# Attention in fp32 parts on one core: low score products of 128 rows, single fp32 copies for the value products, and pieces of the next round issued two steps ahead

## What the reference computes

```python
# fox: forgetting attention
logits = einsum('bhqd,bhkd->bhqk', q, k) * scale + F[..., :, None] - F[:, :, None, :]
p = softmax(where(kpos <= qpos, logits, -inf))
out = einsum('bhqk,bhkd->bhqd', p, v)
# stick-breaking attention
z = einsum('bhqd,bhkd->bhqk', q, k) * scale
after = reverse_cumsum(log_sigmoid(-z)) - log_sigmoid(-z)      # where kpos < qpos
out = einsum('bhqk,bhkd->bhqd', exp(log_sigmoid(z) + after), v)
```

## Time and profile before

| | |
|---|---|
| median of 3 runs | 2871.64 us |
| the profiled execution's own time | 2868.15 us |
| its span, first to last instruction | 2866.0 us |
| mean granted TensorE clock | 0.965 |
| TensorE busy | 95% of the span |
| VectorE, ScalarE, GpSimd busy | 55%, 32%, 33% |
| attention, from the first mask product to the last | 1328.6 to 1982.0 us |

### The profile page before, as it was taken

The page is one execution under the profiler, slowest core; times in us unless marked ns, Lnnn a source line. Parts: engine busy times, 40 slices in busy tenths (PEclk is TensorE's granted clock), DMA queues, the critical chain, the costliest instruction groups (busy, mean ns, idle before and its releaser), DMA issues.

```text
span 2866.0 us, 33315 instructions
## 1 busy us (share of the span) xinstructions
PE 2722.8 (95%) x12938; PEld 2207.3 (77%) x12938; DVE 1579.2 (55%) x1505; ACT 908.4 (32%) x1298; POOL 937.7 (33%) x385
## 2 busy tenths in 40 slices
PE   7999999999999899989999999989999999999998
PEld 4878777878787778867777777777778788888876
DVE  5744455666556633565647466554777714551653
ACT  3411034443343410225445555544223301210211
POOL 2555542323233245531101001000454444444442
PEclk9999999999999999999999999975999999999999
DMA  7222221212121343321101010111111111111111
GB/s 300 68 89 82 103 60 59 71 52 78 45 63 59 114 165 95 118 95 45 36 17 37 31 37 31 37 62 78 37 45 51 44 44 46 50 45 50 51 36 74
DMA packets 54884, 193.61 MB, mean 68 GB/s; under 512 B 6472, under 2 KB 10184, under 8 KB 53616
## 3 DMA queue, kind: packets, MB, share of 16 engines
q1 hardware_dynamic: 39648, 141.08, 14.9%
q10 hardware_dynamic: 15120, 50.90, 5.0%
HBM read 157.84 MB, written 29.92 MB: 66 GB/s over the span
## 4 chain that ended last, share of the span: by engine, by line
PE 79%; DVE 11%; ACT 5%; issue 3%; DMA 1%; DVEq 0%; ACTq 0%; SPq 0%; PEldq 0%; POOL 0%; PEld 0%
PE G L238 51%; PE G L1778 7%; PE G L1838 2%; PE U L1814 2%; PE G L1836 2%; PE S L1031 2%; DVE tiles_in L2399 1%; PE G L1898 1%; DVE tiles_in L2401 1%; PE G L1804 1%; PE S L1804 1%; DVE A_lo L2404 1%; PE U L1063 1%; ACT tiles_in L2352 1%; PE G L1803 1%
## 5 line engine op out<-in xcount | busy, mean ns | idle before, releaser
L264 POOL TENSOR_TENSOR w_hi<-w_raw,ones 128x1024 fp32r<-128x1024 f32 (+1 forms) x141 | 342.5, 2429 | 1167.7 <-PE G L238 984.7
L238 PE MATMUL G<-H_hi,w_hi 128*128 128x512 f32 x1744 | 545.5, 394 | 7.4 <-DVE x L1582 4.7
L238 PE MATMUL G<-H_lo,w_hi 128*128 128x512 f32 x1744 | 538.3, 390 | 0.0
L238 PE MATMUL G<-H_hi,w_lo 128*128 128x512 f32 x1744 | 537.5, 389 | 0.0
L238 PEld LDWEIGHTS G<-H_hi,w_hi 128*128 128x128 f32 x1744 | 324.9, 188 | 80.7 <-issue 6.8
L238 PEld LDWEIGHTS G<-H_lo,w_hi 128*128 128x128 f32 x1744 | 327.9, 188 | 68.8
L238 PEld LDWEIGHTS G<-H_hi,w_lo 128*128 128x128 f32 x1744 | 327.7, 188 | 68.9
L269 POOL TENSOR_TENSOR w_lo<-w_raw,w_hi 128x1024 fp32r<-128x1024 f32 (+1 forms) x141 | 374.6, 2657 | 11.0
L1755 POOL TENSOR_TENSOR w_lo<-w_raw,w_hi 128x1024 fp32r<-128x1024 f32 x24 | 63.8, 2658 | 544.4 <-ACT w_hi L1937 544.4
L2148 DVE TENSOR_TENSOR probsT_lo<-U,probsT_hi 128x512 fp32r<-128x512 f32 (+1 forms) x192 | 101.4, 553 | 170.0 <-ACT probsT_hi L1967 169.0
L238 PE MATMUL G<-A_hi,w_hi 128*128 128x512 f32 x512 | 160.0, 394 | 13.0 <-DVE A_lo L2406 13.0
(11 more groups left out here) (408 smaller groups left out, 4677.1 us busy)
## 6 DMA issues: line engine op xcount, KB each, us to landing
w_raw<-w_in SPq DMA_DIRECT2D x65, 512.0 KB, 3.5
w_raw<-w_up SPq DMA_DIRECT2D x44, 512.0 KB, 3.5
pre_raw<-w_in SPq DMA_DIRECT2D x30, 512.0 KB, 3.6
w_raw<-w_out SPq DMA_DIRECT2D x16, 512.0 KB, 3.7
w_raw<-w_down SPq DMA_DIRECT2D x16, 512.0 KB, 3.5
wm<-w_mod SPq DMA_DIRECT2D x6, 1024.0 KB, 17.0
xT<-xT SPq DMA_DIRECT2D x8, 512.0 KB, 19.2
wm<-w_mod SPq DMA_DIRECT2D x2, 2048.0 KB, 23.6
```

The source lines that it names most:

```text
L238: mm = nc.tensor.matmul(dst[:, n * NB:n * NB + c], w[:, k, :], m[:, k, n * NB:n * NB + c], start=first, stop=last)
L264: eng.tensor_tensor(dst, src, ones.unsqueeze(1).to_broadcast([P, kt, P]), ALU.mult)
```

## The change

It has three parts. **Scores:** each head gets a tile of q low of its own, with zeros in the other head's 64 rows, and the low product takes all 128 rows. Four VectorE instructions write the zeros once, ahead of the rounds. **Value products:** the turned weights and v are copied once, as fp32, by ScalarE, and each block takes one fp32 product of 64 columns. `probs_low`, `v_low` and `values_low` go; `out_of` reads PSUM and writes the output in one instruction. The banks of `U` are free once ScalarE has copied them. **Steps:** SHIFT is 2 in place of 6, so pieces and all that goes by n come four steps later; the last 18 steps have no piece.

```diff
-        TILES, STEPS, SHIFT = 2 * TT, 2 * TT * 2 * HEADS, 6
+        TILES, STEPS, SHIFT = 2 * TT, 2 * TT * 2 * HEADS, 2
...
-            return ([take(f"q_hi{n}{h}", [P, T], F32R) for h in range(2)], take(f"q_lo{n}", [P, T], F32R),
-                    [take(f"k_parts{n}{h}", [P, T], F32R) for h in range(2)], take(f"v_parts{n}", [P, TT, 2, 2, HD], F32R))
+            return [take(f"q_hi{n}{h}", [P, T], F32R) for h in range(2)], [take(f"q_lo{n}{h}", [P, T], F32R) for h in range(2)], \
+                [take(f"k_parts{n}{h}", [P, T], F32R) for h in range(2)], take(f"att_v{n}", [P, TT, P])
...
-                use_u(("p", c), ("dve", "p low", c))
+                use_u(("p", c), ("act", "p copied", c))
...
-                    pe.matmul(z[:, cols], QL[own_rows(hh), t], Ks[hh][own_rows(hh), cols], start=False, stop=tt // 4 != b)
+                    pe.matmul(z[:, cols], Ql[hh][:, t], Ks[hh][:, cols], start=False, stop=tt // 4 != b)
...
                 for c, b0, n in GROUP_AT[g]:
-                    S.wait(pe, "act", "p high", c)
-                    S.wait(pe, "dve", "p low", c)
+                    S.wait(pe, "act", "p copied", c)
                     for b in range(n):
-                        k = b0 + b
-                        if k == 0:
-                            pe.matmul(V[:, at:at + P], pTh[c % 2][:, b, :], v[:, k, hh, :, :].rearrange("p a d -> p (a d)"), start=True, stop=False)
-                        mm = pe.matmul(V[:, at:at + HD], pTl[c % 2][:, b, :], v[:, k, hh, 0, :], start=False, stop=tt == 0)
-                        if k:
-                            mm = pe.matmul(V[:, at:at + P], pTh[c % 2][:, b, :], v[:, k, hh, :, :].rearrange("p a d -> p (a d)"), start=False, stop=k == tt)
+                        mm = pe.matmul(V[:, at:at + HD], pT[c % 2][:, b, :], v[:, b0 + b, own_rows(hh)], start=b0 + b == 0, stop=b0 + b == tt)
...
-            def values_low(g4):
...
+            for n in range(2):
+                for hh in range(2):
+                    other = other_rows(hh)
+                    v.tensor_scalar(SETS[n][1][hh][other, :], SC[other, :], 0.0, None, ALU.mult)
...
-            def v_low(r):
...
-            def probs_low(g):
...
-                do("out", v.tensor_tensor(dst, V.rearrange("p (b a d) -> p b a d", a=2, d=HD)[:, :, 0, :], tb, ALU.add), g4)
+                dst, src = ON[:, t0:t0 + 4, own_rows(hh)], V[:, 0:4 * HD].rearrange("p (b d) -> p b d", d=HD)
                 if x == "f":
-                    me("out", g4)
                     do("row sums", v.reciprocal(rs[:, n0:n0 + 4], rs[:, n0:n0 + 4]), g4)
                     me("row sums", g4)
-                    do("head out", v.tensor_tensor(dst, dst, rs[:, n0:n0 + 4].unsqueeze(2).to_broadcast([P, 4, HD]), ALU.mult), g4)
+                    do("out", v.tensor_tensor(dst, src, rs[:, n0:n0 + 4].unsqueeze(2).to_broadcast([P, 4, HD]), ALU.mult), g4)
+                else:
+                    do("out", v.tensor_copy(dst, src), g4)
```

More of the change, by code:

```diff
@@ L1636, in program @@
         SC = take("rstd12", [P, T])
-        pTh = [take(f"probsT_hi{n}", [P, 4, P], F32R) for n in range(2)]
-        pTl = [take(f"probsT_lo{n}", [P, 4, P], F32R) for n in range(2)]
+        pT = [take(f"probsT{n}", [P, 4, P]) for n in range(2)]
         fsum = [take(f"forget_sums{n}", [P, T]) for n in range(2)]
@@ L1649, in program @@
         left = take("left_over", [P, T + 8])
-        tb = take("values_low", [P, 4, HD])
         dump = take("squares_made", [P, P])
@@ L1698, in program @@
                 for half in range(2):
-                    use_u(("v", 2 * (q - 1) + half), ("dve", "v low", 2 * (q - 1) + half))
+                    use_u(("v", 2 * (q - 1) + half), ("act", "v copied", 2 * (q - 1) + half))
             if s > TILES and s % TILES == 2:
@@ L1787, in scores @@
                 r = g // TILES
-                (Qh, QL, Ks, _), z, w = SETS[r % 2], Z[g % 2], (tt + 1) * P
+                (Qh, Ql, Ks, _), z, w = SETS[r % 2], Z[g % 2], (tt + 1) * P
                 if g == 0:
@@ L1820, in values @@
                 _, hh, tt = tile_of(g)
-                r, at = g // TILES, g % 4 * P
+                r, at = g // TILES, g % 4 * HD
                 v = SETS[r % 2][3]
@@ L1827, in values @@
                 if g % TILES == 0:
-                    S.wait(pe, "dve", "v low", 2 * r + 1)
+                    S.wait(pe, "act", "v copied", 2 * r + 1)
                 for c, b0, n in GROUP_AT[g]:
-                    S.wait(pe, "act", "p high", c)
-                    S.wait(pe, "dve", "p low", c)
+                    S.wait(pe, "act", "p copied", c)
                     for b in range(n):
-                        k = b0 + b
-                        if k == 0:
-                            pe.matmul(V[:, at:at + P], pTh[c % 2][:, b, :], v[:, k, hh, :, :].rearrange("p a d -> p (a d)"), start=True, stop=False)
-                        mm = pe.matmul(V[:, at:at + HD], pTl[c % 2][:, b, :], v[:, k, hh, 0, :], start=False, stop=tt == 0)
-                        if k:
-                            mm = pe.matmul(V[:, at:at + P], pTh[c % 2][:, b, :], v[:, k, hh, :, :].rearrange("p a d -> p (a d)"), start=False, stop=k == tt)
+                        mm = pe.matmul(V[:, at:at + HD], pT[c % 2][:, b, :], v[:, b0 + b, own_rows(hh)], start=b0 + b == 0, stop=b0 + b == tt)
                     S.mark("pe", "values", mm, c)
@@ L1853, in out_turned @@
             def out_turned(r):
-                S.wait(pe, "dve", "out" if X[r % 2] == "s" else "head out", 4 * r + 3)
+                S.wait(pe, "dve", "out", 4 * r + 3)
                 for half in range(2):
@@ L1953, in k_high, with v_copied @@
                 S.mark("act", "k high", ins, q)
-            def v_high(r):
+            def v_copied(r):
                 v = SETS[r % 2][3]
@@ L1959, in v_high, with probs_copied @@
                     S.wait(act, "pe", "v turned", 2 * r + half)
-                    src = bank_of_u(("v", 2 * r + half)).rearrange("p (b h d) -> p b h d", h=2, d=HD)
-                    S.mark("act", "v high", act.activation(v[:, 4 * half:4 * half + 4, :, 0, :], src, ACT.Copy), 2 * r + half)
-            def probs_high(g):
+                    S.mark("act", "v copied", act.activation(v[:, 4 * half:4 * half + 4, :], blocks_of(bank_of_u(("v", 2 * r + half)), 4), ACT.Copy), 2 * r + half)
+            def probs_copied(g):
                 for c, _, n in GROUP_AT[g]:
@@ L1966, in probs_high @@
                     S.wait(act, "pe", "values", c - 2)
-                    S.mark("act", "p high", act.activation(pTh[c % 2][:, 0:n, :], blocks_of(bank_of_u(("p", c)), n), ACT.Copy), c)
+                    S.mark("act", "p copied", act.activation(pT[c % 2][:, 0:n, :], blocks_of(bank_of_u(("p", c)), n), ACT.Copy), c)
             def not_taken(g):
@@ L1984, in probs @@
                 S.mark("act", "made", act.activation(p, p, ACT.Exp, scale=-1.0, bias=mn[:, g % 2, :], accum_out=rs[:, n:n + 1]), g)
-            def values_low(g4):
-                S.wait(act, "pe", "values", last_group(4 * g4 + 3))
-                S.wait(act, "dve", "out", g4 - 1)
-                S.mark("act", "V low", act.activation(tb, V.rearrange("p (b a d) -> p b a d", a=2, d=HD)[:, :, 1, :], ACT.Copy), g4)
             def squares(r, part):
-                S.wait(act, "dve", "out" if X[r % 2] == "s" else "head out", 4 * r + 3)
+                S.wait(act, "dve", "out", 4 * r + 3)
                 for t in range(4 * part, 4 * part + 4):
@@ L2011, in _ @@
                 nxt = s + 1
-                if s >= 5 and s % 4 == 1:
-                    values_low((s - 5) // 4)
                 if 0 <= nxt < STEPS and tile_of(nxt)[0] == "s":
@@ L2016, in _ @@
                 if s >= 1:
-                    probs_high(s - 1)
+                    probs_copied(s - 1)
                 if 0 <= nxt < STEPS:
@@ L2023, in _ @@
                 if n == 0 and 1 <= q <= ROUNDS:
-                    v_high(q - 1)
+                    v_copied(q - 1)
                 if q < ROUNDS:
@@ L2056, in _ @@
                         heads_high(k, A[1][:, k, :].bitcast(F32))
-            values_low(STEPS // 4 - 1)
             for part in range(2):
@@ L2121, in q_low @@
             def q_low(q):
-                Qh, QL = SETS[q % 2][0:2]
+                Qh, Ql = SETS[q % 2][0:2]
                 S.wait(v, "pe", "z", TILES * (q - 1) - 1)
@@ L2126, in q_low @@
                     own = own_rows(hh)
-                    ins = v.tensor_tensor(QL[own, :], qt[own, :], Qh[hh][own, :].bitcast(F32), ALU.subtract)
+                    ins = v.tensor_tensor(Ql[hh][own, :], qt[own, :], Qh[hh][own, :].bitcast(F32), ALU.subtract)
                 do("q low", ins, q)
@@ L2135, in k_low @@
                 do("k low", ins, q)
-            def v_low(r):
[L2138 to L2143, removed]
-            def probs_low(g):
-                for c, _, n in GROUP_AT[g]:
-                    S.wait(v, "act", "p high", c)
```

(15 more changed lines are left out.)

## The result

| | before | after |
|---|---|---|
| median | 2870.7 us (4 runs) | 2758.3 us (2755.55 to 2760.8, 4 runs) |
| ratio, 95% interval | | 0.9609 (0.9592 to 0.9625) |
| profiled execution, span | 2868.15, 2866.0 | 2760.8, 2759.0 |
| mean granted clock | 0.965 | 0.982 |

The kernel is 112 us faster; 2757 was forecast. The timeline's mask products (now L1803) mark the same tiles as the earlier trace rows: 0, 64, 80, 96, 112 and 127.

A forecast was written before the change was run, and what follows sets the result against it. TensorE, busy 95% of the span, was taken as the bound. Scores -54, value products 0, waits -26, moved pieces 0, last round -28 and end -7 sum to -115 us: median 2757 us, range 2738 to 2795.

The forecast's parts named there:

- Scores: Low score products over all 128 rows lose the idle weight-load time: net 7.7 us a round, -54 us over seven rounds.
- Value products: One fp32 product per block in place of two fp32r products: still 0.22 us, set by the loads, so no change.
- Waits: TensorE's waits and the lower clock after some, tiles 0 to 111: 52.6 us becomes 27, left to ScalarE's copies; -26 us.
- Moved pieces: Pieces and weight loads moved by SHIFT keep their cost and pass nothing short of time: net 0 us.
- lower bound of 0.11: Value product time in us if only columns counted; 576 products would then give back 63 us.
- rival D: Slower: the fp32 value product's two passes each wait among transposes, 0.19 us; +104 us, 2976 us in all; chance 0.03.
- The last round: Tiles 112 to 127, without pieces: full clock, ScalarE the bound, 75.3 us becomes 47, -28 us.
- the end: Stretch from 1982.0 to 2018.1, at clock 0.67 with three waits on low parts: 36.1 us becomes 29, -7 us.
- Rival A: The last round stays at 1.2 GHz, gaining 10 us and the end 2: -92 us, 2780 us in all; chance 0.26.
- Rival B: ScalarE takes over: copies at steps 2 to 6 keep waits at 52.6 us or more; -56 us, 2816 us; chance 0.07.
- Rival C: The padded score product waits as before, so the scores part gains nothing: 2813 us in all; chance 0.04.

## Why the prediction was right

The time, the sign and the main stretches came out. The sum of the profile is 1.6 us ahead of tile 0 (7 forecast), 68.9 in tiles 0 to 112 (72), 28.3 in the last round (28), 11.1 at the end (7), and 3.0 us given back after attention: 107 us. After attention the granted clock is 0.98 in place of 0.99, and kernels with the same code there differ by as much.

The near hit in tiles 0 to 112 is in part luck. Taken one after the other by the kernels' own marks, the fp32 products gave 47 us (578.1 to 530.7), the dense scores 43 (to 487.4), and SHIFT 2 took 22 back (to 509.2). Forecast were 26, 54 and 8 back. Waits 21 us too small, scores 11 too large and moved pieces 14 too cheap came to 3 us together.

- **Scores, -54.** The mechanism is as written: starts 0.23 us apart, no idle loads before them. The size was 11 us too high, 43 in place of 54, from the two kernels that differ in this alone (values in fp32, SHIFT 6). Alone in the kernel before, where waits took part of it back, it is 31 in all.
- **Value products, no change.** Right for TensorE, 0.22 us a block. The lower bound of 0.11 is out, and rival D with it.
- **Waits, -26.** The cause was right, the size not: with SHIFT 6 the fp32 products took 47 of the 52.6 us. I charged ScalarE for 27 us left, and it makes few: the waits of TensorE for its copies are 9 us, and the `evac` of step 6, forecast at 1.4 to 2.2 us, costs 0.53 in three "s" rounds and nothing in the "f" rounds. By the work that the experiments leave (525.5 - 43 + 7.6 us), some 19 of the 509.2 us are still waits and low clock. Of these 11.4 went when the low weights moved to n = 14: they are step 12 of the "s" rounds, which the prediction does not name. I had taken 2.46 us for `k_low`, a row without GpSimd beside it, though the same timeline had a product next to GpSimd, of 3.15 us where the same instruction takes 1.23 with nothing beside it (so in the kernel with SHIFT 2 alone):

```profile
1698.18 3.07 POOL L1755 TENSOR_TENSOR w_lo<-w_raw,w_hi 128x1024 fp32r<-128x1024 f32 x1 [21.18 <-ACT w_hi L1937]
...
1699.17 3.15 DVE L2170 TENSOR_TENSOR probs<-probs,left_over 128x1024 f32<-128x1024 f32 x1
```

- **Moved pieces, 0.** This is the step that failed. It costs 22 us here and 30 alone. "Past nothing that is short of time" was wrong twice. The first evacs moved behind the forget sums, which are tied to the step: 7 us. And `k_low`, slowed by GpSimd with either SHIFT, moved to a place where VectorE has less room ahead of the next `evac`: 14 us. The waits, whose gain was forecast too small, hid it.
- **The last round, -28, and the end, -7.** Rival A fell: clock 0.89 and then 1.00. The size of the last round is in part luck. I took full clock and 47 us with ScalarE as the bound; at clock 1.00 the round takes 41.2 to 43.2 us (three of the kernels above), and in the kernel after 10.2 us at 1.2 GHz made up the rest. In the profiled executions neither part alone brings the clock back: 0.55 with dense scores, 0.58 with fp32 values, 0.63 with 64 rows in the kernel after, against 0.82 to 1.00 with both. The four executions of fp32 values that were not profiled had a higher clock, so how far that part goes alone is not settled.
- **Rival A's sum** has a slip: 34.3 us doubled and taken by 75.3 / 81.6 is 63 us and not 65, so it should stand some 2 us lower.
- **Rival B** has a true core: ScalarE is at 77% in the last round. In the other rounds it does not bound. **Rival C** is out.

## What to carry to other kernels

Between 512-column products of 128 rows, one of 64 rows costs TensorE about 0.19 us more at each change of rows (0.42 us from start to start and not 0.23). Zeros, or a term too small to matter, in the other half cost no time. When steps are moved by a number, list what is tied to another number on the same in-order engine, and for each wait what work its engine has ahead of it at the new place: here that was worth more than the 8 us that the move was about. Parts of a change should be timed apart even where the whole is a success: this one is 22 us faster without its third part.

## What the runs showed of the hardware

- GpSimd's 2.4 us of subtraction on SBUF adds about 2 us to a VectorE instruction of two tensors that begins while it runs: `k_low` 2.46 to 4.54 us, a product 0.83 to 2.74, `q_low` 2.44 to 4.50. What it adds is about what is left of GpSimd's: 2.06 us were left when that product began, and it grew by 1.91. Moving it moves the 2 us to the next such instruction. The other way round, the half of `q_low` that began 0.3 us ahead of GpSimd took its 1.21 us as ever, and GpSimd took 3.09 in place of 2.4.
- The granted clock of the stretch without pieces went with both changes together, in the profiled executions: at 1.2 GHz for 48 to 72 us of its 65 to 77 with 64-row or two-part products, and for 0 to 17 us of its 41 to 48 with both replaced, between kernels that issue the same products there. Why it differs between those stays open.
- A fp32 product with 64 columns costs what one with 128 does: both leave two records and are 0.22 us apart.
